# Recurrent layer of a two-block transformer kernel: head outputs with tokens on partitions, norm per token, transposes ahead of the output projection

## What is computed

```python
q, key, v = silu(q_raw), (1 - lb) * sigmoid(-z), i_raw         # from x @ w_in, per head
b = cumsum(log_f, within a chunk)
q_dec, k_dec = q * exp(b), key * exp(-b)
a = where(causal, q_dec @ k_dec.T, 0)                           # inside a chunk
o_intra = a @ v
states = scan(decay_c * state + kv_c)                           # over the 8 chunks
o_inter = q_dec @ states
o = o_intra + o_inter
o = o * rsqrt(mean(o * o, over the head's 128 features) + 1e-6) * norm_g
y = o @ w_out
```

## Time and profile before

| | us |
|---|---|
| median of 3 runs | 2250.44 (2246.43 to 2251.75) |
| profiled execution, its own time | 2248.31 |
| its span | 2246.5 |
| TensorE busy | 2145.9 (96%) |
| VectorE busy | 1277.9 (57%) |
| ScalarE busy | 885.9 (39%) |

### The profile page before, as it was taken

The page is one execution under the profiler, slowest core; times in us unless marked ns, Lnnn a source line. Parts: engine busy times, 40 slices in busy tenths (PEclk is TensorE's granted clock), DMA queues, the critical chain, the costliest instruction groups (busy, mean ns, idle before and its releaser), DMA issues.

```text
span 2246.5 us, 29430 instructions
## 1 busy us (share of the span) xinstructions
PE 2145.9 (96%) x11034; PEld 1744.7 (78%) x11034; DVE 1277.9 (57%) x1995; ACT 885.9 (39%) x1298; POOL 69.3 (3%) x63
## 2 busy tenths in 40 slices
PE   7979999999999999999998999999989998999997
PEld 6747778888877888888876788888777876888886
DVE  6986464434455566666667642344568886433444
ACT  4324242222226565565562431242345524322322
POOL 1000300000030000000000000000000000000000
PEclk9989999999999999999999899999999998999998
DMA  4001312232232122122221223222112221222221
GB/s 168 30 11 57 113 60 105 85 106 94 77 129 85 67 66 85 66 84 66 84 75 52 75 95 111 94 93 94 57 57 75 75 75 65 103 94 94 93 96 55
DMA packets 31508, 183.38 MB, mean 82 GB/s; under 512 B 5184, under 2 KB 5568, under 8 KB 12736
## 3 DMA queue, kind: packets, MB, share of 16 engines
q1 hardware_dynamic: 27504, 176.18, 22.9%
q10 hardware_dynamic: 3024, 6.00, 0.8%
q0 software_dynamic: 896, 0.06, 0.0%
HBM read 180.06 MB, written 2.10 MB: 81 GB/s over the span
## 4 chain that ended last, share of the span: by engine, by line
PE 82%; DVE 10%; DVEq 4%; ACT 2%; issue 1%; ACTq 0%
PE ps L569 12%; PE ps L571 12%; PE ps L570 12%; PE ps L1059 5%; PE ps L1061 5%; PE ps L1060 5%; PE ps L1115 2%; PE ps L1116 2%; PE ps L1117 2%; PE ps L690 2%; PE ps L599 1%; PE ps L601 1%; PE ps L600 1%; DVE f_run L2606 1%; PE ps L630 1%
## 5 line engine op out<-in xcount | busy, mean ns | idle before, releaser
L1285 ACT ACTIVATE w_hi<-raw 128x2048 fp32r<-128x2048 f32 (+1 forms) x122 | 226.0, 1853 | 296.6 <-PE ps L571 220.1
L569 PE MATMUL ps<-x_hi,w_lo 128*128 128x512 f32 x816 | 317.6, 389 | 0.5 <-DVE y L2203 0.3
L571 PE MATMUL ps<-x_hi,w_hi 128*128 128x512 f32 x816 | 317.4, 389 | 0.0
L570 PE MATMUL ps<-x_lo,w_hi 128*128 128x512 f32 x816 | 317.4, 389 | 0.0
L1726 DVE TENSOR_TENSOR w_lo<-raw,w_hi 128x2048 fp32r<-128x2048 f32 (+3 forms) x116 | 259.2, 2235 | 93.9 <-ACT w_hi L1285 93.6
L1059 PE MATMUL ps<-x_hi,w_lo 128*128 128x512 f32 x544 | 218.2, 401 | 2.9 <-DVE w_lo L2373 2.4
L1061 PE MATMUL ps<-x_hi,w_hi 128*128 128x512 f32 x544 | 212.5, 391 | 0.0
L1060 PE MATMUL ps<-x_lo,w_hi 128*128 128x512 f32 x544 | 211.8, 389 | 0.0
L569 PEld LDWEIGHTS ps<-x_hi,w_lo 128*128 128x128 f32 x816 | 153.2, 188 | 33.0 <-issue 0.7
L571 PEld LDWEIGHTS ps<-x_hi,w_hi 128*128 128x128 f32 x816 | 153.2, 188 | 31.8
L570 PEld LDWEIGHTS ps<-x_lo,w_hi 128*128 128x128 f32 x816 | 153.2, 188 | 31.7
(11 more groups left out here) (454 smaller groups left out, 3980.7 us busy)
## 6 DMA issues: line engine op xcount, KB each, us to landing
raw<-w_attn_in SPq DMA_DIRECT2D x32, 1024.0 KB, 4.9
raw<-w_gate_up SPq DMA_DIRECT2D x22, 1024.0 KB, 4.9
raw<-w_up_a SPq DMA_DIRECT2D x16, 1024.0 KB, 4.9
raw<-w_down_a SPq DMA_DIRECT2D x16, 1024.0 KB, 4.9
raw<-w_up_h SPq DMA_DIRECT2D x16, 1024.0 KB, 4.9
raw<-w_down_h SPq DMA_DIRECT2D x16, 1024.0 KB, 4.9
raw<-w_hgrn_in SPq DMA_DIRECT2D x8, 1024.0 KB, 4.9
raw<-w_down SPq DMA_DIRECT2D x8, 768.0 KB, 4.3
```

Source lines behind the costliest of these rows:

```text
L569: pe.matmul(o, w_lo[:, slot, a:a + P], hi[:, k, :], start=k == 0, stop=False)
L570: pe.matmul(o, w_hi[:, slot, a:a + P], lo[:, k, :], start=False, stop=False)
L571: last = pe.matmul(o, w_hi[:, slot, a:a + P], hi[:, k, :], start=False, stop=k == st.kc - 1)
L1285: act.activation(w_hi[:, slot, 0:width], raw[:, slot, 0:width], ACT.Copy).then_inc(whi_ready, 1)
```

## The change

The output of a head is computed with tokens on partitions. In L1201 and L1209 the two operands change places: the masked a and q_dec are loaded as weights, v_htok and the state are streamed. The inter-chunk products write 64 partitions each and stream 128 columns. The output of step 8 is in bank 7 too.

The sum of squares over a head's features is now a sum along the free axis. VectorE takes it (`sum_squares`, a reduce of 128 x 512 to 128 x 4) at the end of its step and gives `sq_used`; L1217 is gone. ScalarE's square root and VectorE's reciprocal are over 128 x 4. The scaling, without the gain, makes hg_tok (`scale_head`), not at the end of the step but in the next one, behind the w_lo of 1024 columns and ahead of the mask; it gives `oh_ready`.

TensorE turns hg_tok with four transposes into bank 5 (`turn_head`), between tile 0 and the wait for `dec_ready` of the next step, and waits for `oh_ready` ahead of them. xo_hi and xo_lo are made from that bank with the gain as their scale. Since the kv products write bank 5, TensorE waits for the last xo_lo ahead of them. After step 8 head 7 is turned between the seventh and the last chunk of the output projection.

```diff
@@ -182,11 +182,11 @@
     f_cum = at("f_cum", BIG_AT + 16 * KB, [2, T])
     q_dec = at("q_dec", BIG_AT + 20 * KB, [2, T])
     k_dec = at("k_dec", BIG_AT + 24 * KB, [2, T])
-    hg_o = at("hg_o", BIG_AT + 32 * KB, [HG_HEADS, T])
     xo_lo = at("xo_lo", BIG_AT + 32 * KB, [HG_HEADS, T], f32r)
     xo_hi = at("xo_hi", BIG_AT + 48 * KB, [HG_HEADS, T], f32r)
     f_run = at("f_run", Y_AT, [T])
     f_start = at("f_start", Y_AT + 2 * KB, [T])
+    hg_tok = at("hg_tok", Y_AT + 4 * KB, [TB, P])
     k_tok = at("k_tok", Y_AT + 12 * KB, [TB, P])
     v_htok = at("v_htok", Y_AT + 14 * KB, [TB, P])
 
...
@@ -1159,11 +1159,12 @@
             def step(hd, par, project, attend):
 
                 a, old = hd - 1, 1 - par
-                o_bank = O_BANK if project else O_LAST
                 if project:
                     hgrn_tile(hd, par, 0, range(DC))
                 else:
                     out_part(0, range(0, 4))
+                if not (isinstance(hd, int) and hd < 2):
+                    turn_head(hd - 2)
                 if attend:
                     pe.wait_ge(dec_ready, a + 1)
                     if first(a):
@@ -1184,7 +1185,8 @@
                     out_part(0, range(4, 5))
                 if attend:
                     pe.wait_ge(ht_ready, a + 1)
-                    pe.wait_ge(root_ready, SK["head0"] + a)
+                    if not first(a):
+                        pe.wait_ge(xlo_ready, XB["hgrn_out"] + a)
                     for c in range(7):
                         half = slice(CHUNK * (c % 2), CHUNK * (c % 2) + CHUNK)
                         last = pe.matmul(ps[:, 5 + c % 2, (c // 2) * P:(c // 2 + 1) * P], k_tok[half, c // 2, :],
@@ -1194,27 +1196,32 @@
                     if not project:
                         out_part(0, range(5, 6))
                         out_part(1, range(0, 2))
-                    elif not (isinstance(a, int) and a == 0):
+                    if not first(a):
                         pe.wait_ge(oh_ready, a)
                     for b in range(TB):
                         sl = slice(b * P, (b + 1) * P)
-                        pe.matmul(ps[:, o_bank, sl], v_htok[:, b, :], tmp[:, 3, sl], start=b == 0, stop=False,
+                        pe.matmul(ps[:, O_BANK, sl], tmp[:, 3, sl], v_htok[:, b, :], start=b == 0, stop=False,
                                   skip_group_check=True)
                 if project:
                     hgrn_tile(hd, par, 2, range(DC - 1 if attend else DC))
                 if attend:
                     pe.wait_ge(st_ready, a + 1)
                     for c in range(1, 8):
-                        sl = slice(c * CHUNK, (c + 1) * CHUNK)
-                        last = pe.matmul(ps[:, o_bank, sl], state[:, c, :], q_dec[:, old, sl], start=False, stop=c == 7,
-                                         skip_group_check=True)
+                        half, at_ = CHUNK * (c % 2), (c // 2) * P
+                        last = pe.matmul(ps[half:half + CHUNK, O_BANK, at_:at_ + P], q_dec[:, old, c * CHUNK:(c + 1) * CHUNK],
+                                         state[:, c, :], start=False, stop=c >= 6, skip_group_check=True)
                     last.then_inc(oh_done, 1)
                     if project:
                         hgrn_tile(hd, par, 2, (DC - 1,))
                     else:
                         out_part(1, range(2, 3))
-                    pe.wait_ge(sq_ready, SB["head0"] + a + 1)
-                    pe.matmul(ps[:, 5, :], ones, sq[:, 0, :], start=True, stop=True).then_inc(sq_used, 1)
+
+            def turn_head(n):
+
+                pe.wait_ge(oh_ready, n + 1)
+                for b in range(TB):
+                    last = pe.transpose(ps[:, 5, b * P:(b + 1) * P], hg_tok[:, b, :], ident)
+                last.then_inc(oht_done, 1)
 
             def out_part(c, chunks):
                 for k in chunks:
@@ -1257,9 +1264,11 @@
             read_out(st, STAGES["hgrn_out"])
             step(HG_HEADS, 0, False, True)
             out_part(1, range(3, 6))
-            out_part(0, range(6, DC))
-            out_part(1, range(6, DC))
-            pe.wait_ge(oh_ready, HG_HEADS)
+            out_part(0, range(6, DC - 1))
+            out_part(1, range(6, DC - 1))
+            turn_head(HG_HEADS - 1)
+            out_part(0, range(DC - 1, DC))
+            out_part(1, range(DC - 1, DC))
             norm_and_ffn("h", "hgrn_out", "up_h", "down_h")
 
         @block.scalar
@@ -1678,7 +1687,7 @@
                     act.activation(k_tok[:, :, :].rearrange("p a c -> p (a c)"), ps[:, 3, :], ACT.Copy)
                     act.activation(v_htok[:, :, :].rearrange("p a c -> p (a c)"), ps[:, 4, :], ACT.Copy) \
                        .then_inc(ht_ready, 1)
-                if project and not (isinstance(hd, int) and hd < 2):
+                if not (isinstance(hd, int) and hd < 2):
                     head_hi(hd - 2)
                 if project:
                     act.wait_ge(tile_done, st.tile0 + 3 * hd + 2)
@@ -1688,19 +1697,19 @@
                         split_next(hd, par, i, 1)
                 if attend:
                     act.wait_ge(oh_done, a + 1)
-                    act.activation(sq[:, 0, :], ps[:, SUM if project else O_LAST, :], ACT.Square).then_inc(sq_ready, 1)
+                    act.activation(sq[:, 0, :], ps[:, SUM, :], ACT.Square).then_inc(sq_ready, 1)
                 if project:
                     act.wait_ge(tile_done, st.tile0 + 3 * hd + 3)
                     act.activation(hg_v[:, par, :], banks[2], ACT.Copy).then_inc(tile_free["act"], 1)
                 if attend:
                     act.wait_ge(sq_used, SB["head0"] + a + 1)
                     act.wait_ge(rstd_ready, SK_ROOT["head0"] + a)
-                    act.activation(root[:, :], ps[:, 5, :], ACT.Sqrt, bias=eps[:, 0:1], scale=1.0 / P) \
-                       .then_inc(root_ready, 1)
+                    act.activation(root4, mean4, ACT.Sqrt, bias=eps[:, 0:1], scale=1.0 / P).then_inc(root_ready, 1)
 
             def head_hi(hd):
-                act.wait_ge(oh_ready, hd + 1)
-                act.activation(chunk(xo_hi, hd), chunk(hg_o, hd), ACT.Copy).then_inc(xhi_ready, 1)
+                act.wait_ge(oht_done, hd + 1)
+                act.activation(chunk(xo_hi, hd), ps[:, 5, :], ACT.Copy, scale=gains[:, ds(GAIN_AT["g_hgrn"] + hd, 1)]) \
+                   .then_inc(xhi_ready, 1)
 
             step(0, 0, 0, True, False)
             step(1, 1, 0, True, True)
@@ -1709,7 +1718,6 @@
                 step(2 * i + 1, 1, i, True, True)
             split_hi(STAGES["hgrn_out"], 0, 0)
             step(HG_HEADS, 0, 0, False, True)
-            head_hi(HG_HEADS - 2)
             head_hi(HG_HEADS - 1)
             norm_and_ffn("h", "hgrn_out", "up_h", "down_h", 1, None)
 
@@ -2560,23 +2568,30 @@
 
             def head_lo(hd):
                 dve.wait_ge(xhi_ready, XB["hgrn_out"] + hd + 1)
-                tt(chunk(xo_lo, hd), chunk(hg_o, hd), chunk(xo_hi, hd).bitcast(f32), ALU.subtract).then_inc(xlo_ready, 1)
-
-            def finish(a, bank):
+                stt(chunk(xo_lo, hd), ps[:, 5, :], gains[:, ds(GAIN_AT["g_hgrn"] + hd, 1)], chunk(xo_hi, hd).bitcast(f32),
+                    ALU.mult, ALU.subtract).then_inc(xlo_ready, 1)
+
+            def sum_squares(a):
+                dve.wait_ge(sq_ready, SB["head0"] + a + 1)
+                dve.tensor_reduce(mean4, sq[:, 0, :].rearrange("p (b f) -> p b f", b=TB), AX.X, ALU.add).then_inc(sq_used, 1)
+
+            def scale_head(a):
                 dve.wait_ge(root_ready, SK["head0"] + a + 1)
-                dve.reciprocal(rstd[:, :], root[:, :]).then_inc(rstd_ready, 1)
-                settle()
-                stt(chunk(hg_o, a), ps[:, bank, :], gains[:, ds(GAIN_AT["g_hgrn"] + a, 1)], rstd[:, :], ALU.mult,
-                    ALU.mult).then_inc(oh_ready, 1)
+                dve.reciprocal(rstd4, root4).then_inc(rstd_ready, 1)
+                settle()
+                tt(hg_tok[:, :, :], ps[:, SUM, :].rearrange("p (b f) -> p b f", b=TB),
+                   rstd4.unsqueeze(2).to_broadcast([P, TB, P]), ALU.mult).then_inc(oh_ready, 1)
 
             def step(hd, par, project, attend):
                 a, old = hd - 1, 1 - par
                 if project:
                     split_next(hd, par, 1 if first(hd) else 0)
+                if not (isinstance(hd, int) and hd < 2):
+                    scale_head(hd - 2)
                 if attend:
                     dve.wait_ge(a_done, a + 1)
                     tt(tmp[:, 3, :], ps[:, 2, :], a_mask[:, :], ALU.mult).then_inc(a_ready, 1)
-                    if project and not (isinstance(hd, int) and hd < 2):
+                    if not (isinstance(hd, int) and hd < 2):
                         head_lo(hd - 2)
 
                     dve.wait_ge(kv_done, a + 1)
@@ -2607,8 +2622,8 @@
                     tt(q_dec[:, par, :], hg_q[:, par, :], f_cum[:, par, :], ALU.mult)
                     settle()
```

(12 more changed lines are left out.)

## The result

The changed kernel takes 2305.9 us (median of 4 runs, 2299.98 to 2306.25), the kernel before 2250.05 (4 runs): 1.0244 times as long, 95% interval 1.0232 to 1.0256. The forecast was 2309, the range 2291 to 2323. The profiled execution took 2306.25 us, its span is 2304.4.

A forecast was written before the change was run, and what follows sets the result against it. A ring of waits through VectorE and TensorE was taken to bound the 23.54 us step. 48.6 + 10.0 + 0.8 - 0.3 = 59.1 us on 2248.31 gives 2307.4; the median, 2.1 higher, gives 2309.5, rounded to 2309; range 2291 to 2323.

The forecast's parts named there:

- The ring: Recurrent layer: waits from k_dec through TensorE and VectorE to the next k_dec set the 23.54 us step; TensorE spare 0.27.
- The wait: TensorE at turn_head waits for oh_ready; L1173 starts 6.70 us behind k_dec instead of 0.81, each step grows 5.9 us.
- the queue: Ahead of the scaled head: squares' sum, table load and root, w_hi, w_lo, reciprocal, scaling; done 6.21 us after k_dec starts.
- Rival 3: Table load goes ahead of its wait in the loop, as in step 1; 1.28 us saved a step, 2301 to 2298; chance 0.10.
- The clock: Low clock behind each TensorE gap, on L1173, L1179 and tile 1; 1.7 to 2.6 us a gap, 2.2 taken.
- Step 8 and the tail: Last step and layer end: wait 7.8 us, 10.0 with clock, kv 0.8, tail -0.3.
- kv's wait: Step 8: kv products also wait for xo_lo of head 6; 0.8 us (0 to 1.1).
- the last idle time: Layer end: TensorE idle for head 7's two conversions, about 1.6 us.
- The sum: Whole kernel: 48.6 for steps 2 to 7, then 10.0 + 0.8 - 0.3, in all 59.1 us longer.
- The rule on table loads: ScalarE's root: a drain of about 1380 ns on each switch would add 9.7 us; the sum follows the trace, without it.
- Rival 6: Not slower: no wait at turn_head, ring unchanged, gain at most 1.9 us, 2248.5; chance 0.05.
- what was given for them: Inter-chunk products in their new form on TensorE: fourteen passes take 1.1 to 2.0 us, no difference taken.

The follow-up runs named there:

- short reciprocal: Kernel before with the reciprocal L2567 over 4 of its 512 columns, output not the layer's, only its time of use; 2246.5 us, ratio 0.9985.
- turn under cover: Changed kernel with turn_head behind L1203 into bank 4, and root, scaling, xo_hi and xo_lo reordered, so kv waits for neither conversion; 2251.3 us, ratio 1.000.
- gap filled: Changed kernel with 24 more products of 512 columns, results unread, on TensorE ahead of turn_head; 2290.8 us, ratio 1.0186.
- turn behind tile 1: Changed kernel with turn_head behind tile 1 instead of ahead of the wait for dec_ready, still in bank 5; 2276.0 us, ratio 1.0127.

## Why the prediction was right, point by point

- *The ring sets the step, not TensorE's 96%.* Right, and shown from both sides: taking 3.2 us off VectorE (short reciprocal) or 1.0 us off TensorE (turn under cover) left 23.55 us, taking 2.0 us off the ring as well gave 22.0. But TensorE's load is the next limit, and near: in the kernel before it allows 23.01 us, so TensorE had 0.53 us to spare and not the 0.27 of the prediction.
- *The wait.* The transposes were put at 6.26 us behind the start of k_dec and start at 6.16. With the clock up (gap filled) the step is 29.31; 23.54 + 5.9 = 29.4 was the reckoning. Each link of the queue held: the table load 0.10 behind the sum, the root 0.30, w_hi 1.04, w_lo, the scaling at the 0.69 of the earlier trace rows and not at 1.07. (The 1.07 us of L1981, which the prediction calls the price of a strided write, belong to an operation that reads both operands with a stride and writes without one.)
- *Rival 3, in one step.* In step 2 the transposes start 4.90 us behind k_dec (1671.75). That root belongs to ScalarE's step 1, outside the loop, where the load already went ahead of the wait in the earlier trace rows. Six like steps was the wrong count; five and one would have taken off 1.3 us. Timelines of ScalarE and TensorE:

```profile
1665.68 1.28 ACT L1707 ACT_TABLE_LOAD   x1
1673.13 0.30 ACT L1707 ACTIVATE by_token<-by_token,eps 128x4 f32<-128x4 f32 x1 [6.18 <-DVE by_token L2576]
```

```profile
1676.65 1.11 PE L1223 MATMUL ps<-consts,hg_tok 128*128 128x128 f32 x4 [6.14 <-DVE hg_tok L2582]
```

- *The clock.* Mechanism right, size off: 2.2 us a step was taken, and the difference of the changed kernel to the filled one is 2.70, 2.11, 1.76, 1.57, 1.50 and 1.48, 11.1 us in all instead of 13.2. The low stretch is 6.8 us in each of these steps, but a part of it (3.1 us in the windows shown) lies in the gap, where it costs nothing. This and the one shorter wait, for the most part, bring steps 2 to 7 to 44.4 us instead of 48.6.
- *Step 8 and the tail.* 11.7 us instead of 10.5. Wait 8.08 - 0.81 + 0.44 = 7.7 (7.8 forecast), clock 2.1 (2.2; the low stretch was 10.2 us here), kv's wait 1.18 (0.8), the last idle time 1.56 (1.6). What I left out: with head 7 turned in front of the last chunks, chunk 0's tiles of the output projection end only 6 products ahead of the next slab instead of 12, and TensorE waits 1.11 us for its w_lo (L1115). The kernel before reaches the same product without idle time:

```profile
1834.57 0.43 PE L1115 MATMUL ps<-xo_hi,w_lo 128*128 128x512 f32 x1
```

- *The sum.* 44.4 + 11.7 = 56.1 in the layer against 59.1, and 55.8 between the medians. Steps 2 to 7 were 4.2 us too dear and step 8 with the tail 1.2 us too cheap, so the total is nearer than its larger part, and that is luck.
- *The rule on table loads.* The load ends at 1736.62 and the activation starts at 1736.64: the changed kernel, too, shows nothing of the drain of about 1380 ns that the Trainium skill (ScalarE: Activation LUTs, What ACT_TABLE_LOAD costs) adds.
- *Rival 6, the only one that is not slower*, is what the turn under cover shows with another order: no wait at the transposes, ring unchanged, no gain. The forecast put its gain at 1.9 us at most, the kernel shows none (1.000).

## What to carry to other kernels

Removing work from an engine that is nearly full gains nothing if the time is set by a ring of dependences through two engines. To find the ring, go from an instruction to the one that released it, and on, until the same instruction of the step before is reached; then shorten a link of that ring. A lighter operation that moves to another engine takes its place in that engine's order: count everything that stands in front of it, on each engine it passes, from the last thing that it waits for, and place its consumer where other work still lies ahead. A step in the layout may pay only once the order has been made for it: here the same arithmetic gave 2306 and 2238 us in two orders.

## What was not expected of the hardware

- In the layer, gaps of TensorE of 3.88 us and more were always followed by a low clock (3.88, 4.4, 5.0, 7.1 and 8.0 us among them). Shorter ones mostly were not: neither the 1.65 us of each step nor the 2.58 us of step 8 with the gap filled, nor the 2.09 us of step 2 with the turn under cover. But with the turn behind tile 1 the clock fell in three steps of six, behind gaps of 1.93 to 2.03 us, and not behind 1.92. The low stretches were 3.4, 6.8 or 10.2 us long. What decides stays open.
- The inter-chunk products in their new form (128 x 64 weights into alternating halves of the partitions, 128 columns streamed) take 1.09 us for 14 passes instead of 1.67 with 64 columns, at the lower bound of what was given for them. Timelines of TensorE before and after:

```profile
1706.48 1.67 PE L1209 MATMUL ps<-q_dec,state 128*128 128x64 f32 x14
```

```profile
1756.62 1.09 PE L1211 MATMUL ps<-state,q_dec 128*64 128x128 f32 x14
```

The Trainium skill (TensorEngine Tiling (Array Packing), Tiling Modes) says that different tiles can load weights and multiply in parallel; 0.08 us a pass with twice the columns fits that. The loads of the weights are shorter too, 0.137 us instead of 0.192 in the median, and no run here separates the two.
